# Mixer stages of a two-layer hybrid decoder on one core: projection tiles issued in pieces between small products, another order of branch tiles, norm roots on four rows, a convolution tap on ScalarE

## The reference, cut to what matters

```
u = rmsnorm(h);  z = u @ w_in                       # one wide projection feeds all four mixers
GLA: vector decay q,k,v                  -> rmsnorm per head (128) * silu(gate)
RET: rope, scalar decay                  -> rmsnorm per head (128) * silu(gate)
GDN: causal_conv(4 taps), silu; l2norm(q), l2norm(k);
     u,w = triangular_solve(...)  (chunked delta rule) -> rmsnorm per head * silu(gate)
SSD: causal_conv(4 taps)+bias, silu; 8 heads -> (y * silu(z)), rmsnorm per group (256)
out = sum_n sigmoid(mg_n) * (branch_n @ w_branch_n) @ w_out;  h = h + out
```

## Time and profile before

| | us |
|---|---|
| median of three runs | 2736.98 |
| profiled execution | 2750.4 |
| its span | 2748.3 |
| PE busy | 2462.7 (90%) |
| DVE busy | 1628.5 (59%) |
| ACT busy | 1074.4 (39%) |

### The profile page before, as it was taken

The page is one execution under the profiler, slowest core; times in us unless marked ns, Lnnn a source line. Parts: engine busy times, 40 slices in busy tenths (PEclk is TensorE's granted clock), DMA queues, the critical chain, the costliest instruction groups (busy, mean ns, idle before and its releaser), DMA issues.

```text
span 2748.3 us, 38217 instructions
## 1 busy us (share of the span) xinstructions
PE 2462.7 (90%) x14436; PEld 2124.5 (77%) x14436; DVE 1628.5 (59%) x2112; ACT 1074.4 (39%) x1450; POOL 178.8 (7%) x247
## 2 busy tenths in 40 slices
PE   8899868868999989889778879899999999999996
PEld 7788758857699978779678766678878778787786
DVE  4453554264366463544553443387887878778785
ACT  3322321112033343324221121166766667567563
POOL 0210101111000000211011201000000000000000
PEclk8889879778899999999889688799999999999999
DMA  5224321021345432323311122288988889889871
GB/s 192 93 82 141 117 74 50 31 97 39 137 146 166 164 129 93 105 103 115 125 54 47 59 70 72 90 309 301 333 294 317 303 300 331 294 299 321 299 282 74
DMA packets 122566, 456.43 MB, mean 166 GB/s; under 512 B 14056, under 2 KB 14474, under 8 KB 120018
## 3 DMA queue, kind: packets, MB, share of 16 engines
q1 hardware_dynamic: 118818, 432.66, 44.6%
q0 software_dynamic: 3632, 22.12, 2.2%
HBM read 443.72 MB, written 11.00 MB: 165 GB/s over the span
## 4 chain that ended last, share of the span: by engine, by line
PE 77%; DVE 11%; issue 5%; ACT 4%; DMA 1%; POOL 1%; DVEq 0%; SPq 0%; ACTq 0%; POOLq 0%
PE ps L715 9%; PE ps L717 8%; PE ps L716 8%; PE ps L762 5%; DVE weights_low L2220 4%; PE ps L1265 4%; PE ps L1267 3%; PE ps L1266 3%; PE ps L1287 3%; PE ps L1288 3%; PE ps L1289 3%; PE ps L1238 3%; PE ps L756 2%; PE ps L896 2%; DMA ring<-in_stream 1%
## 5 line engine op out<-in xcount | busy, mean ns | idle before, releaser
L715 PE MATMUL ps<-u_high,tiles_high 128*128 128x288 f32 x1688 | 535.1, 317 | 2.6 <-DVE arena L1712 2.6
L716 PE MATMUL ps<-u_low,tiles_high 128*128 128x288 f32 x1688 | 521.3, 309 | 0.0
L717 PE MATMUL ps<-u_high,tiles_low 128*128 128x288 f32 x1688 | 519.1, 307 | 0.0
L1688 DVE TENSOR_TENSOR tiles_low<-ring,tiles_high 128x1024 fp32r<-128x1024 f32 x238 | 291.7, 1229 | 268.7 <-ACT tiles_high L1346 267.6
L715 PEld LDWEIGHTS ps<-u_high,tiles_high 128*128 128x128 f32 x1688 | 340.8, 202 | 12.7 <-issue 6.7
L1346 ACT ACTIVATE tiles_high<-ring 128x1024 fp32r<-128x1024 f32 x238 | 250.7, 1054 | 245.9 <-DMA ring<-in_stream 155.9
L716 PEld LDWEIGHTS ps<-u_low,tiles_high 128*128 128x128 f32 x1688 | 341.0, 202 | 0.6
L717 PEld LDWEIGHTS ps<-u_high,tiles_low 128*128 128x128 f32 x1688 | 340.3, 202 | 0.0
L2220 DVE TENSOR_TENSOR weights_low<-expert_ring,weights_high 128x1024 fp32r<-128x1024 f32 x288 | 334.3, 1217 | 4.9 <-ACT weights_high L1597 2.2
L1265 PE MATMUL ps<-weights_high,u_high 128*128 128x512 f32 (+1 forms) x768 | 297.6, 388 | 23.2 <-DVE weights_low L2220 22.6
L2220 DVE TENSOR_TENSOR weights_low<-ring,weights_high 128x1024 fp32r<-128x1024 f32 x240 | 280.1, 1217 | 42.9 <-ACT weights_high L1597 41.8
(11 more groups left out here) (381 smaller groups left out, 3377.6 us busy)
## 6 DMA issues: line engine op xcount, KB each, us to landing
ring<-in_stream SPq DMA_DIRECT2D x530, 512.0 KB, 4.2
expert_ring<-in_stream SPq DMA_DIRECT2D x288, 512.0 KB, 5.5
arena<-in_state POOLq DMA_DIRECT2D x8, 1024.0 KB, 5.2
state_s<-arena POOLq DMA_DIRECT2D x8, 1024.0 KB, 4.2
const<-in_const SPq DMA_DIRECT2D x1, 2052.5 KB, 12.0
arena<-in_const POOLq DMA_DIRECT2D x2, 832.0 KB, 4.9
h<-in_x SPq DMA_DIRECT2D x1, 1152.0 KB, 5.1
y<-acc POOLq DMA_DIRECT2D x1, 1152.0 KB, 4.4
```

The costliest lines, as they stand in the source:

```text
L715: mm(out, hi[k], uh[:, k, :], start=k == 0, stop=False)
L716: mm(out, hi[k], ul[:, k, :], start=False, stop=False)
L717: last = mm(out, lo[k], uh[:, k, :], start=False, stop=k == KD - 1)
L1688: tt(t_low[:, q % HELD, :], ring[:, (t % RING) * TILE:(t % RING + 1) * TILE], t_high[:, q % HELD, :].bitcast(F32), ALU.subtract).then_inc( ...
```

## The change

1. Pieces of tiles. PE can begin the first tile of a slot early (`begin`), issue it in units (three products of one 128-row block, or one product of a `br` tile) with `drip`, and issue the rest in `fill`. This is done in `prep`, in every `core` (one unit after each pair of 4-column products), in each of the seven inverse levels (three units between L1062's and L1069's successors), and in `states` (four units ahead, then one after every second group). One more unit call stands in GDN's loop over the samples, whose slot holds no tile.
2. The order. In the table mg(n) moves behind z: mg(1) stands before br(1), mg(2) before br(2). A table MG_STAGE puts mg(1) into GDN and mg(2), mg(3) into SSD, so tiles per stage go from 24, 22, 12 (RET, GDN, SSD) to 16, 22, 20; GLA keeps 20. SLOTS is rewritten.
3. Roots on four rows. The sums go to 4 rows (32 rows for GDN's q and k), ACT's root and DVE's reciprocal work on 4x288 (32x288), and PE spreads the result over 128 rows again in PSUM (`spread_rows`); the final multiplication reads PSUM. `states` now waits for `o_final`, the end of that multiplication.
4. The first tap of both convolutions is made by ACT (`tap`), two blocks ahead; the buffer `cbuf` has three places instead of two.

The core of the diff:

```diff
         out += z(1) + mg(0)
-        out += br(0) + z(2) + mg(1)
-        out += br(1) + z(3) + mg(2)
-        out += br(2) + mg(3)
+        out += br(0) + z(2)
+        out += mg(1) + br(1) + z(3)
+        out += mg(2) + br(2) + mg(3)
@@ SLOTS, one line of four; MG_STAGE
-    [3, 2, 2, 3, 3, 2, 2, 2, 2, 3],
+    [2, 1, 1, 1, 2, 1, 2, 2, 2, 2],
+MG_STAGE = [0, 2, 3, 3]
@@ PE
+            def product_units(out, x):
+                q = Q_OF[T_OF[x]]
+                pe.wait_ge(tile_low, q + 1)
+                for k in range(KD):
+                    hi, lo = [y[:, q % HELD, P * k:P * k + P] for y in (t_high, t_low)]
+                    mm(out, hi, u_high[:, k, :], start=k == 0, stop=False)
+                    mm(out, hi, u_low[:, k, :], start=False, stop=False)
+                    last = mm(out, lo, u_high[:, k, :], start=False, stop=k == KD - 1)
+                    ...
+                    yield
             def fill(L, n, s):
+                begun = tiles.finish()
                 for x in FILL[L][n][s]:
-                    stream_tile(x)
+                    if x != begun:
+                        stream_tile(x)
@@ core: outputs
                             if b == NSEQ - 1:
                                 last.then_inc(o_ps, 1)
+                        tiles.drip(1)
@@ out_sums, spread_rows, states
-                        last = mm(bank(M + b)[:, 0:TOK], C("ones"), tmp4[:, b, :], start=True, stop=True)
+                for b in range(4):
+                    r = b // 2 if n == SSD else b
+                    last = mm(bank(M)[0:4, 0:TOK], C("row_of", 3 - r, 7 - r), tmp4[:, b, :], start=b == 0, stop=b == 3)
+            def spread_rows(L, n):
+                pe.wait_ge(row_ready, 5 * L + ROWS_AT[n] + 1)
+                for b in range(2 if n == SSD else 4):
+                    last = mm(bank(M + b)[:, 0:TOK], C("ident")[0:4, b:b + 1].to_broadcast([4, P]), rs4[0:4, 0, :],
+                              start=True, stop=True)
+                last.then_inc(row_ps, 1)
-                pe.wait_ge(ort_ready, m + 1)
+                spread_rows(L, n)
                 pe.wait_ge(o_taken, L * NHEAD + HBASE[n] + HEADS[n])
+                if slot is not None:
+                    begin(L, n, slot)
+                    tiles.drip(4)
+                pe.wait_ge(o_final, m + 1)
@@ GDN, inverse levels
                     last.then_inc(p_ps, 1)
-                    fill(L, GDN, 16 + 2 * lv)
+                    begin(L, GDN, 17 + 2 * lv)
+                    tiles.drip(3)
                     pe.wait_ge(p_ready, 7 * L + lv + 1)
@@ ACT: conv
+                def tap(b):
+                    ...
+                    if b >= 3:
+                        act.wait_ge(conv_ready, 14 * L + ci - 2)
+                    A(cbuf[:, b % 3, 0:312], zblk(n, b)[:, 0:312], ACT.Identity, scale=PVc("conv_w", ci),
+                      bias=PVc("conv_b", ci)).then_inc(tap_ready, 1)
@@ DVE: out_norm, conv
-                V.reciprocal(rs4[:, 0:w, :], rs4[:, 0:w, :]).then_inc(dve_step, 1)
-                dve.wait_ge(dve_step, steps.next())
+                V.reciprocal(rs4[0:4, 0, :], rs4[0:4, 0, :]).then_inc(row_ready, 1)
+                dve.wait_ge(row_ps, 5 * L + ROWS_AT[n] + 1)
-                    last = tt(o4, g4, rs4, ALU.mult)
+                    last = tt(o4, g4, ps_t[:, M:M + 4, 0:TOK], ALU.mult)
-                    ts(out, src[:, 0:312], wv[:, 0, ci:ci + 1], PVc("conv_b", ci), ALU.mult, ALU.add).then_inc(dve_step, 1)
-                    dve.wait_ge(dve_step, steps.next())
+                    dve.wait_ge(tap_ready, 14 * L + ci + 1)
```

More of the change, by code:

```diff
@@ L170, in constants @@
     c["slot_col"] = np.arange(P)[:, None] * 1.0
+    c["row_of"] = np.tile(np.arange(7)[None, :] == 3, (P, 1)) * 1.0
     c["ret_decay"] = c.pop("ret_decay")
@@ L230 @@
 Q_OF = {t: q for q, t in enumerate(SPLIT)}
+ROWS_AT = [0, 1, 3, 4]
+QK_ROWS = 2
 NORM_AT = {0: 0, 1: 1, 2: 2, 3: 3, 5: 4}
@@ L796, in prep @@
                                   start=k == 0, stop=k == KD - 1)
-                last.then_inc(small_ps, 1)
+                        if (b, k) == (2, KD - 1):
+                            last.then_inc(small_ps, 1)
+                        if k % 3 == 2:
+                            tiles.drip(1)
+                tiles.finish()
                 pe.wait_ge(glr_ready, L + 1)
@@ L802, in prep @@
                 last.then_inc(gk_ps, 1)
-                for b in range(4, ZBLOCKS[0]):
+                for b in range(5, ZBLOCKS[0]):
                     stream_tile(("z", L, 0, b))
@@ L899, in outputs @@
                                 last.then_inc(o_ps, 1)
+                        tiles.drip(1)
                 for hh in range(HEADS[n]):
                     gh = L * NHEAD + HBASE[n] + hh
+                    begin(L, n, slot + hh)
                     if n != GLA:
@@ L916, in core @@
                 if n != GLA:
+                    begin(L, n, slot + HEADS[n])
                     outputs(HEADS[n] - 2)
@@ L957, in states @@
                                 last.then_inc(masked_used, 1)
+                        if b % 2:
+                            tiles.drip(1)
             def gla(L):
@@ L1004, in gla @@
                 fill(L, GLA, 16)
-                states(L, GLA)
+                states(L, GLA, 17)
                 fill(L, GLA, 17)
@@ L1082, in gdn @@
                 pe.wait_ge(state_in, 16 * (4 * L + GDN + 1))
+                begin(L, GDN, 30)
                 for b in range(NSEQ):
+                    tiles.drip(1)
                     for hh in range(4):
@@ L1114, in gdn @@
                 fill(L, GDN, 38)
-                states(L, GDN)
+                states(L, GDN, 39)
                 for s in range(39, NSLOT[GDN]):
@@ L1133, in ret @@
                 fill(L, RET, 7)
-                states(L, RET)
+                states(L, RET, 8)
                 for s in range(8, NSLOT[RET]):
@@ L1917, in conv @@
                         fill(L, n, b - 1)
+                    if n == GDN and b == nb - 1:
+                        dve.wait_ge(ort_ready, 5 * L + QK_ROWS + 1)
+                        V.reciprocal(rs4[0:32, 0, :], rs4[0:32, 0, :]).then_inc(row_ready, 1)
                 finish(nb - 1)
```

117 lines of the change are left out of this document (80 added, 37 removed), and 4 rows, old and new, of the table SLOTS.

## The result

The changed kernel takes 2819.9 us (median of 4 runs, 2808.4 to 2822.4) against 2737.0 for the kernel before: ratio 1.028, interval 1.025 to 1.032. It is slower by 83 us; the forecast was 2625. The profiled execution took 2821.8 us, 71 more than that of before (which was itself 13 us above the median).

The account below looks back on a forecast made before the run. It took idle PE (some 197 us), in the convolutions a chain through four engines, and the low clock as the losses to win back. Layer 0's -58 and layer 1's -54 gave 2737 - 112 = 2625 us, range 2560 to 2690.

Parts of the forecast that it names:

- (a): GDN's convolution, now with 8 mg and 2 br tiles, PE setting the pace for mg tiles: 59.0 us against 59.9.
- (b): GDN from q, k to the first level: 43.3 us to 30.5; in SSD, transposes to scores: 21.0 to 37.1.
- The last block's turn: End of GDN's convolution: the chain once more, with ACT's tanh table load and two multiplications, +7 us.
- (c): GDN's seven inverse levels, 71.9 us before: units cover waits, levels 9.05 us each, 63.4 in all.
- (d): GDN's rest behind the levels: 65.7 us to 59.0; in SSD, the last part with `states` waiting: 22.8 to 29.3.
- turn of the chain: Convolutions: PE's br tile, ACT's high and tanh, DVE's split and take, PE again; about 14 us a turn.
- Core: SSD's core, 39.3 us before: two more tiles, 6 us of clock won back, squares 3.3 later; 40.3 us.
- the three signs: What would show the forecast wrong: levels over 10 us apart, clock at 0.85, or SSD over 140 us.
- Units don't lift the clock: Rival, chance 0.10: idle waits stay around the units, the clock terms of 41 us are lost; 2666 us.
- Slower: Rival, chance 0.04: each inverse level waits for its tile's low part; at 10 us a level, 2753 us.
- The clock stays up nearly everywhere: Rival, chance 0.20: half of the 200 us of low clock comes back, 55 us more gain; 2570 us.
- The chain moves along: Rival, chance 0.12: mg tiles tie ACT's takes to the blocks, each convolution keeps two 14 us turns; 2681 us.

Follow-up runs that it names:

- order_only: The kernel before with the new branch order, stages and slots alone, no units, rows or tap: 2714.3 us, ratio 0.988.
- units_by_two: The changed kernel with units among 4-column products issued two at a time at every second sequence: 2772.3 us, ratio 1.011.
- units_by_four: The changed kernel with units among 4-column products issued four at a time at every fourth sequence: 2750.3 us, ratio 1.004.
- no_units: The changed kernel with no units at all, every tile issued whole at its slot: 2738.5 us, ratio 0.998.
- old_norms_no_units: The changed kernel without any units and with the output norms of before; new order, q and k roots on rows and tap stay: 2685.0 us, ratio 0.981.
- block_units: The changed kernel with units only in blocks (inverse levels, head of states), none among 4-column or 16-column products: 2739.5 us, ratio 0.998.

## Why the prediction was wrong

*The step that failed is the price of units among 4-column products.* I had them save 9.13 - 6.50 = 2.6 us a tile in GLA, 6 us in each of GDN and SSD, and bring the clock back, and gave a cost of the change no bound at all. They cost 81 us. I read two rows of the same tiles at two clocks and inferred that units keep it up. They don't. In the changed kernel the clock fell at 253.9 us in RET, within a run of groups, and PE had not been idle in the 21.35 us before. Its windows there:

```profile
232.54:253.89 21.35, 21.35 (x119) 0.98 0.42 149
253.89:263.29 9.40, 9.40 (x51) 0.64 0.04 6
```

Before the change the same stage kept 1.00 from the transposes to the sums. But that the units made it fall isn't shown: with whole tiles in the new order the stage is at 0.91 over the same part (order_only), PE busy throughout, and with units at 0.89. So in RET the clock went with the new order. In GDN's outputs it stayed down through the groups, where it rises within a whole tile (see units_by_two, units_by_four).

A row for a unit beside a small product was at hand: the first product of a tile behind 4-column ones takes 0.40 us in the kernel before, the others 0.30. It says that the change isn't free, not what it costs: behind whole-array products, where the mixing costs nothing, the first one takes 0.38. The Trainium skill's rule that the prediction named ("HAM oscillation — how this bites in real kernels", idle gaps of PE) would not have told this loss either: here the clock fell with none. What the prediction drew from it, that filling busy stretches gives nothing, was nearer to the result than the forecast.

Of the 195 us between 2625 and 2820, the units are 81, the output norms 53, and the blocks 1. The other 60 are gains that came out smaller than forecast.

*Output norms.* I booked 2.1 us a stage for the spreading products, 1.3 to 3 us here and there for waits. They cost 53 us, 6.6 us a stage. From the sums to the next stage (both layers, no_units against old_norms_no_units) the rows add 16.5, 6.9, 10.2 and 13.9 us in GLA, RET, GDN and SSD. The mis-sized terms are SSD's +3.4 for the last multiplication and the missing turn in the others: PE to DVE to PE, each behind tiles in a queue. And the gain from shorter reciprocals was nil, as the old ones were off the path. The reciprocal itself is as forecast, by source line:

```profile
L1965 DVE RECIPROCAL arena<-arena x8: 1932/1933/1942, 191.0 to 1733.3; 4x288 f32<-4x288 f32 x8
L2025 DVE RECIPROCAL arena<-arena x2: 1941/1942/1942, 378.1 to 1412.7; 32x288 f32<-32x288 f32 x2
```

Four, 32 or 128 rows of 288 columns take the same time; four times the columns take 7.35 us.

*Prep and GLA.* Prep is +0.6 where I had -3.5 (bounds 0 and -7), and GLA 127.2 us against 119.6. From the transposes to the sums GLA takes 100.3 us in layer 1 with mixing and 96.2 in block_units, 96.1 in no_units. Layer 0 doesn't show it: 103.0 with mixing, 95.9 in block_units, but 103.1 in no_units, as the clock moves this stretch too (0.85 in no_units, 0.93 in block_units). From the sums on it takes 26.1 against 21.5 us before, with the norms on rows.

*RET, 112.6 against 91.5.* The order alone does its part inside the stage: from transposes to sums 46.4 (order_only) against 60.8 us. Mixing put 5.3 of it back, the late `states` and the clock behind it another 10.

*GDN.* (a) 67.3 against 59.0, (b) 41.2 against 30.5: I let the clock's spread in as a bound only, and it went past that bound (38). With no tile between, the decays and products run at 1.2 GHz (clock 0.62). Taking the tiles out gave 2 of the 13 us. The last block's turn was 8.74 us of idle PE (I had 7):

```profile
377.08 5.72 PE L821 MATMUL ps<-arena,ring 128*128 128x288 f32 x16 [7.06 <-DVE arena L1819]
...
393.63 1.11 PE L914 MATMUL ps<-const,arena 128*128 128x128 f32 x4 [8.74 <-DVE arena L2135]
```

(c) levels 9.52 us apart, not 9.05. The blocks of three and five units take longer than 1.2 and 2.0 us, and 0.5 of wait stays. (d) 83.8 against 59.0: up to the sums it takes 58.1 us where the kernel before took 47.6, the mixing at the lower clock; behind them 25.7 against 18.1, the norms on rows.

*SSD.* Conv 24.8 (25.5 forecast) and (b) 35.0 (37.1) were right: no branch tile, no turn of the chain. Core 48.3 (40.3) is the mixing at full clock, four runs of eight groups, 8 us. The forecast's own sum was wrong there too: 39.3 + 6.5 - 6 + 3.3 is 43.1, which would have made it 2631 and not 2625 over two layers. (d) 32.3 (29.3).

*Signs and rivals.* Two of the three signs that the forecast named for being wrong came: the clock was under 0.85 in the mixers, and SSD took 140.4 us. "Units don't lift the clock" (2666) was the one nearest, but it priced units at nothing. "Slower" had the wrong mechanism: no level waits for `low`. The chance of 0.04 for that side rested on one mechanism of my own making, with no room for a cost of the mixing itself. "The clock stays up nearly everywhere" is refuted by the earlier trace rows against the windows after: over all mixer stages 0.83 in both layers, where it was 0.84 and 0.86. "The chain moves along" didn't come: SSD's convolution has no turn left, and GDN's has the two waits that the forecast had (7.06 and 8.74 us). Without units and with the old output norms the change gives 52 us, less than half of my 112. They are the order and the roots of q and k, which the prediction had right in kind, and a part that is the clock behind the levels.

## What to carry to other kernels

Fill a busy in-order PE with whole tiles between small products, not with pieces among them, above all where the small products use half of the array: count the changes of kind, here 0.25 us each at full clock and 0.38 at 1.2 GHz. A new step that goes PE, DVE, PE costs a turn through both queues, so shorten work only where something waits for it. In GDN's outputs the clock, low behind small products, came back within a whole tile and not within its pieces; but before you read a difference of clock as the work of an edit, look at runs without that edit.

## What the hardware showed that I had not expected

- From a tile's products (fp32r) to fp32 ones that also use the whole array, the weight load runs 0.12 us ahead, and the mixing costs nothing; beside 64-column weights it doesn't, and a group costs 0.22 to 0.25 us more, even behind 256 columns.
- The same products of GDN behind the levels, up to the sums, ran at a mean clock of 0.78 or of 0.57 in kernels that differ elsewhere, with a whole tile and no idle time ahead of them in both (38.0 against 48.1 us). What decides it is open.
- A reciprocal of 4x288 takes as long (1.93 us) as one of 128x288 (1.95).
